# First attention of a two-block transformer kernel: a turned tile is copied ahead of the exponentials, a weight unit is split sooner, and the first weight load comes in two halves

## The reference, cut to what matters

```python
def dsa_mixer(h, w_in, kv_norm_g, w_uk, w_uv, w_o, rel_bias):
    q, c, qi, ki, wi = jnp.split(h @ w_in, ATT_IN_SPLITS, axis=-1)   # 16 heads of 64, latent 128
    c = rms_norm(c, kv_norm_g)
    q_lat = jnp.einsum('bshd,hdc->bshc', q, w_uk) * ATT_SCALE
    # for each of two blocks of 128 queries:
    dots = jax.nn.relu(jnp.einsum('bqhd,bsd->bqhs', qi_b, ki))       # 8 index heads
    score = jnp.einsum('bqh,bqhs->bqs', wi_b, dots)
    _, idx = lax.top_k(where(causal, score, -inf), 64)
    logits = q_lat_b . c_sel + rel_bias[t5_bucket(dist)]             # the 64 chosen keys only
    p = softmax(where(dist >= 0, logits, -inf))
    o_lat = p @ c_sel
    o = jnp.einsum('bshc,hcv->bshv', o_lat, w_uv)
    return o @ w_o
```

## Time and profile before

| | |
|---|---|
| Median of 3 runs | 875.04 us |
| The profiled execution's own time | 875.46 us |
| Its span, first to last instruction | 873.3 us |
| TensorE matmuls busy | 856.1 us (98%) |
| VectorE busy | 684.2 us (78%) |
| ScalarE busy | 474.7 us (54%) |
| GpSimd busy | 136.5 us (16%) |
| Mean granted TensorE clock | 0.996 |
| Share of TensorE in the chain that ended last | 93% |

### The profile page before, as it was taken

How to read it: one execution, slowest core, us unless ns; L and a number is a source line. 1 busy time by engine, 2 the same in 40 slices (tenths; PEclk the granted TensorE clock), 3 DMA queues, 4 the chain that set the end, 5 groups by cost and what they waited for, 6 DMA issues and landing times.

```text
span 873.3 us, 17948 instructions
## 1 busy us (share of the span) xinstructions
PE 856.1 (98%) x7016; PEld 816.8 (94%) x7016; DVE 684.2 (78%) x1074; ACT 474.7 (54%) x699; POOL 136.5 (16%) x154
## 2 busy tenths in 40 slices
PE   6999999999999998899999999999999999999998
PEld 5998999999999996699999999989899999999998
DVE  4897789898877797677666677677758998997884
ACT  7783455565443465765555444463367557645741
POOL 6230100014311000000000122232203223013000
PEclk9999999999999998999999999999999999999999
DMA  9755767769997450165665666566445544454652
GB/s 347 261 196 191 271 213 249 241 234 308 255 273 182 152 178 12 32 207 186 206 194 193 205 196 194 172 208 200 165 142 172 169 157 158 155 183 149 199 184 97
DMA packets 46960, 167.86 MB, mean 192 GB/s; under 512 B 5776, under 2 KB 5920, under 8 KB 46640
## 3 DMA queue, kind: packets, MB, share of 16 engines
q1 hardware_dynamic: 40896, 146.82, 50.7%
q0 software_dynamic: 5856, 20.00, 8.0%
q10 hardware_dynamic: 144, 0.15, 0.1%
HBM read 165.50 MB, written 1.44 MB: 191 GB/s over the span
## 4 chain that ended last, share of the span: by engine, by line
PE 93%; DVE 3%; ACT 2%; issue 1%; DMA 1%; POOL 0%; DVEq 0%; SPq 0%; ACTq 0%
PE bank L548 26%; PE bank L552 26%; PE bank L553 25%; PE bank L621 5%; PE bank L639 2%; PE bank L791 1%; PE bank L915 1%; PE bank L925 1%; PE bank L874 1%; PE bank L876 1%; PE bank L875 1%; DMA plain<-plain_w 1%; DVE lt L1736 1%; PE bank L782 1%; PE bank L803 0%
## 5 line engine op out<-in xcount | busy, mean ns | idle before, releaser
L1377 DVE TENSOR_TENSOR wlo<-raw,whi 128x1024 fp32r<-128x1024 f32 x260 | 319.5, 1261 | 91.8 <-ACT whi L1010 91.6
L552 PE MATMUL bank<-xl,whi 128*128 128x256 f32 x1328 | 370.1, 279 | 0.0
L553 PE MATMUL bank<-xh,wlo 128*128 128x256 f32 x1328 | 368.8, 278 | 0.0
L548 PE MATMUL bank<-xh,whi 128*128 128x256 f32 x1310 | 368.3, 281 | 0.0
L1010 ACT ACTIVATE whi<-raw 128x1024 fp32r<-128x1024 f32 x260 | 265.9, 1053 | 147.4 <-PE bank L553 135.8
L548 PEld LDWEIGHTS bank<-xh,whi 128*128 128x128 f32 x1310 | 246.0, 188 | 8.8 <-issue 6.8
L552 PEld LDWEIGHTS bank<-xl,whi 128*128 128x128 f32 x1328 | 249.6, 188 | 0.3
L553 PEld LDWEIGHTS bank<-xh,wlo 128*128 128x128 f32 x1328 | 249.5, 188 | 0.0
L552 PE MATMUL bank<-hlo,whi 128*128 128x256 f32 x512 | 141.9, 277 | 0.0
L553 PE MATMUL bank<-hhi,wlo 128*128 128x256 f32 x512 | 141.5, 276 | 0.0
L548 PE MATMUL bank<-hhi,whi 128*128 128x256 f32 x506 | 140.0, 277 | 0.0
(11 more groups left out here) (291 smaller groups left out, 1083.5 us busy)
## 6 DMA issues: line engine op xcount, KB each, us to landing
raw<-weights SPq DMA_DIRECT2D x260, 512.0 KB, 4.4
ada_raw<-ada_w POOLq DMA_DIRECT2D x24, 512.0 KB, 4.6
plain<-plain_w SPq DMA_DIRECT2D x16, 512.0 KB, 6.6
relB<-rel_scratch POOLq DMA_DIRECT2D x8, 256.0 KB, 7.3
bl<-rpb_in POOLq DMA_DIRECT2D x32, 64.0 KB, 3.4
x<-x_in SPq DMA_DIRECT2D x4, 256.0 KB, 6.3
cond<-cond_in POOLq DMA_DIRECT2D x1, 1024.0 KB, 7.5
cx<-ctx_in POOLq DMA_DIRECT2D x1, 1024.0 KB, 7.4
```

Source lines behind the costliest of these rows:

```text
L548: mmul(dst, hi, rh, start=start, stop=False)
L552: mmul(dst, hi, rlo, start=False, stop=False)
L553: return mmul(dst, lo, rh, start=False, stop=stop)
L1377: V_.tensor_tensor(wlo[:, sl], raw[:, sl], whi[:, sl].bitcast(F32), ALU.subtract)\
```

## The change

- **Start.** Plain chunk 0 is loaded in two halves with semaphores of their own, each 256 KB: the first behind x tiles 0 and 1, the second behind x tiles 2 and 3. TensorE waits for the first half at k = 0 and for the second at k = 4.
- **Ahead of the attention.** VectorE splits the two chunks of the second q unit while it would wait for the index weights and for the small transposition; before, it split them after the scores of block 0. Top-k rounds, scores and bank reads are put in another order behind it: three rounds of block 1 instead of two come before the loop. ScalarE's one-column Exp comes before its last split, not after it.
- **In the loop.** ScalarE's `copy_turned(g-2)` comes before `softmax(g)`. VectorE's top-k rounds are 1, 2, 1, 1 (the last after `queries(3)`) in g = 0, 1, 2, 2; before they were 1, 2, 1, 2. TensorE does three k steps of the output projection's first chunk at g = 12 and two at g = 13; before it did five at g = 13.

```diff
--- before.py
+++ after.py
@@ -270,7 +270,7 @@
         OUTS = (bank[7], bank[0])
 
 
-        names = """xg_ready plain_used cols_loaded consts_loaded rel_loaded w_hi_ready w_lo_ready chunk_used bank_emptied
+        names = """xg_ready plain_head plain_used cols_loaded consts_loaded rel_loaded w_hi_ready w_lo_ready chunk_used bank_emptied
             act_bank_emptied ada_used ada_summed cond_loaded cond_ready ones_ready x_hi_ready x_lo_ready x_squared tile_added
             squares_summed sum_in_psum root_ready rstd_ready dve_chain act_chain pool_chain rel_psum rel_table
             rel_stored rel_bias_loaded mask_ready bias2_ready k_full v_full kv_emptied gate_ready conv_ready rg_bank_read lam_parts lam_ready
@@ -336,8 +336,10 @@
                     sp.dma_start(raw[:, (2 * r + c) % 4], w[q * 8 + 2 * r + c]).then_inc(s_raw[(2 * r + c) % 4], 16)
 
             load_x(0)
-            load_plain(0)
-            for j in range(1, 4):
+            sp.dma_start(plain[:, 0, 0:CH // 2], plain_w[0][:, 0:CH // 2]).then_inc(S_["plain_head"], 16)
+            load_x(1)
+            sp.dma_start(plain[:, 0, CH // 2:CH], plain_w[0][:, CH // 2:CH]).then_inc(s_plain[0], 16)
+            for j in range(2, 4):
                 load_x(j)
             for n in range(1, 4):
                 load_plain(n)
@@ -614,8 +616,13 @@
                     pe.wait_ge(S_["bank_emptied"], f - 1)
                 for c in range(2):
                     n = N0[name] + 2 * unit + c
-                    pe.wait_ge(s_plain[n % NR], 16 * (n // NR + 1))
+                    if n:
+                        pe.wait_ge(s_plain[n % NR], 16 * (n // NR + 1))
                     for k in range(DT):
+                        if n == 0 and k == 0:
+                            pe.wait_ge(S_["plain_head"], 16)
+                        if n == 0 and k == DT // 2:
+                            pe.wait_ge(s_plain[0], 16)
                         if first_wait is not None and c == 0:
                             first_wait(k)
                         mm = mmul(b[:, c * S:(c + 1) * S], plain[:, n % NR, k * P:(k + 1) * P], rhs(k),
@@ -836,8 +843,10 @@
                     logits(g)
                 if g == 2:
                     q_last(1)
+                if g == NG:
+                    att_out_first(0, 0, 3)
                 if g == NG + 1:
-                    att_out_first(0, 0, 5)
+                    att_out_first(0, 3, 5)
                 if 2 <= g < NG + 2:
                     turn(pt, 3, "probs_ready", "turned_copied", "probs_turned", g - 2)
                 if g == NG + 2:
@@ -1183,8 +1192,8 @@
                     act.wait_ge(S_["dots_used"], g - 3)
                 A(rl[:, g % 4, 0:2 * n], DOTS[g % 4][:, 0:2 * n], ACT.Relu).then_inc(S_["dots_relu"], 1)
             ahead(U0["q"] + 2)
+            A(den[:, 0, 0:1], eps[:], ACT.Exp)
             ahead(U0["ukuv"])
-            A(den[:, 0, 0:1], eps[:], ACT.Exp)
 
             for j in range(4):
                 if j < 3:
@@ -1225,10 +1234,10 @@
                     half(U0["att_out"], 0)
                 if g == NG + 1:
                     half(U0["att_out"], 1)
+                if 2 <= g < NG + 2:
+                    copy_turned(g - 2)
                 if g < NG:
                     softmax(g)
-                if 2 <= g < NG + 2:
-                    copy_turned(g - 2)
                 if g >= 3:
                     act.wait_ge(S_["outs_full"], g - 2)
                     b, t0, nt, nk = GROUPS[g - 3]
@@ -1663,10 +1672,12 @@
                         .then_inc(S_["c_normed"], 1)
                 full(u)
                 emptied(V_.tensor_tensor(ci[:, 2 * j:2 * j + 2], two(bank[(F0["lat"] + j) % 2]), wide(R[:, 0]), ALU.mult))
+            half(U0["q"] + 1, 0)
             dve.wait_ge(S_["wi_psum"], 1)
             V_.scalar_tensor_tensor(wit[:], OUTB[0:2 * H_IDX, 0:S], IDX_SCALE, R[0:2 * H_IDX, 0], ALU.mult, ALU.mult)\
                 .then_inc(S_["wi_rows"], 1)
 
+            half(U0["q"] + 1, 1)
             dve.wait_ge(S_["wi_cols"], 1)
             ch.link(V_.tensor_copy(wi[:].rearrange("p b h -> p (b h)"), OUTB[:, S:S + QB * H_IDX]))
             def scores(g):
@@ -1705,23 +1716,22 @@
                 emptied(V_.scalar_tensor_tensor(qT[:, 2 * j:2 * j + 2], two(b), ATT_SCALE, wide(R[:, 0]), ALU.mult, ALU.mult))
             for g in range(4):
                 scores(g)
-            ahead(U0["q"])
-            topk(0, 0, 2)
+            topk(0, 0, 4)
             queries(0)
             dve.wait_ge(S_["c_hi"], 1)
             V_.tensor_tensor(cnl[:], cn[:], cnh[:].bitcast(F32), ALU.subtract).then_inc(S_["c_lo"], 1)
-            topk(0, 2, 4)
+            topk(0, 4, 5)
             ahead(U0["q"] + 1)
-            topk(0, 4, 8)
+            topk(0, 5, 8)
+            scores(4)
             queries(1)
+            scores(5)
             ahead(U0["q"] + 2)
-            scores(4)
-            scores(5)
+            scores(6)
             queries(2)
-            scores(6)
             scores(7)
             ahead(U0["ukuv"])
-            topk(1, 0, 2)
+            topk(1, 0, 3)
 
             def read_logits(g):
                 b, t0, nt, nk = GROUPS[g]
@@ -1763,13 +1773,13 @@
                 if 1 <= g <= NG:
                     norm_probs(g - 1)
                 if g == 0:
-                    topk(1, 2, 3)
+                    topk(1, 3, 4)
                 if g == 1:
-                    topk(1, 3, 5)
+                    topk(1, 4, 6)
                 if g == 2:
-                    topk(1, 5, 6)
+                    topk(1, 6, 7)
                     queries(3)
-                    topk(1, 6, 8)
+                    topk(1, 7, 8)
                 if g == 9:
                     half(U0["att_out"], 0)
                 if g == NG + 2:
```

## The result

The changed kernel takes **868.01 us** (median of 4 runs, 867.67 to 868.39) against 874.76 (4 runs, 874.32 to 875.98) of the kernel before on the same chip: 6.75 us less, a ratio of 0.992 with a 95% interval of 0.9905 to 0.9935. The forecast was 868.3. The profiled execution took 868.39 us with a span of 866.2; before they were 875.46 and 873.3.

What follows compares the result with a forecast made beforehand. TensorE was taken as the bound, so only its idle time and clock could be won. Terms 0.5 - 0.1 + 0.4 + 3.5 + 2.7 - 0.4 + 0.15 = 6.75 gave 868.3 us for the median, range 867.0 to 872.4.

Steps and rivals of the forecast that it cites:

- the mask: In the attention loop: mask 1.4 us sooner, PE's wait of 0.39 for it gone, +0.4 us.
- kT and the table: Ahead of the values: table load hidden in a ScalarE gap, kT copies 1.4 sooner, wait of 0.45 gone, +0.5 us.
- The copy ahead of the exponentials: In the attention loop: the transposition's waits for pT fall from 3.8 to 0.3 us, +3.5 (bounds 1.9 and 3.8).
- The added wait, costed at 0: ScalarE at g = 2: softmax(2) behind the copy ends near 336.3, VectorE wants it at 337.5; slack 1.2 us, cost 0.
- The clock: In the attention: with less PE idle time it keeps 2.4 GHz throughout, +2.7 us (bounds 0 and 2.9).
- the clock falls anyway: Rival: PE still idles in the attention, some 7 us run at 1.2 GHz, 871.0 us; chance 0.12.
- The wait for queries(3): PE's wait for the last q bank grows from 0.92 to 1.0 us, -0.1 (bounds -0.5 and +0.4).
- The end of the loop: Last hcl stands behind a VectorE split formerly finished in time; PE's wait grows 0.36 to 0.8, -0.4 us.
- The first load: At the start: halved load lets PE begin up to 0.7 us sooner, gain +0.15 (bounds 0 and 0.7).
- only the difference to POOL can be had: At the sum of squares: POOL runs 5.51 to 15.47, PE arrives at 15.69; that difference less 0.1 is the gain.
- The copy isn't what the transposition waits for: Rival: softmax(2) ends late, the transposition waits for VectorE's pt, wait only 1.90 to 0.7, 872.2 us; chance 0.08.
- The loop closes over one group: Rival: the next transposition needs the softmax behind the copy, 3.95 us a group, clock down, 881.3 us; chance 0.03.

Runs made afterwards that it cites:

- Experiment 1: Kernel before with only ScalarE's copy of the turned tile put ahead of the exponentials: 869.65 us against 874.94, ratio 0.9941.
- Experiment 5: Changed kernel again, 868.06 us; with its first weight load whole again, 868.50; with all five k steps at g = 13 again, 868.65.
- experiment 6: Changed kernel with five matmuls of the output projection's second unit cut in two by columns: 867.89 us, ratio 0.9924.
- experiment 2: Kernel before with only VectorE's whole list of the changed kernel (splits in two gaps, new order of rounds): 871.24 us, ratio 0.9962.
- experiment 3: Kernel before with 14 unused matmuls filling PE's wait ahead of the transposition of group 2: 873.86 us, ratio 0.999.
- experiment 4: Kernel before with only the first weight load in two halves: 873.76 us, ratio 0.9989.
- 7: Changed kernel with VectorE's queries(3) one top-k round sooner: 867.62 us against 867.61 of the changed kernel beside it.
- experiment 8: Changed kernel with the column cuts, q_last's two subtractions moved from VectorE to GpSimd, and rounds and queries(3) moved forward: 868.89 us, ratio 0.9937.

## Why the prediction was right

The mechanism was right where most of the gain lies, in the copy's place, the mask, kT and the table. The sum fits partly by luck, as the end of this section shows.

The prediction's steps against PE's timeline, each as how much sooner an instruction comes, before minus after. A step's gain is the difference to the one above:

| Instruction (PE's, the root ScalarE's) | before | after | sooner | step | forecast |
|---|---|---|---|---|---|
| first cnh matmul | 318.75 | 318.37 | 0.38 | start of the kernel 0.38 | 0.15 |
| first matmul of the values | 322.16 | 321.09 | 1.07 | kT and table 0.69 | 0.5 |
| mask of g = 3 | 335.42 | 334.72 | 0.70 | queries(3) -0.37 | -0.1 |
| mask of g = 4 | 338.14 | 336.97 | 1.17 | mask 0.47 | 0.4 |
| turn(2) | 341.14 | 338.21 | 2.93 | copy, first 1.76 | 1.75 |
| mask of g = 7 | 349.74 | 344.02 | 5.72 | clock 2.79 | 2.7 |
| mask of g = 11 | 359.46 | 352.98 | 6.48 | copy, later 0.76 | } 1.75 and |
| last waiting k step | 369.41 | 361.66 | 7.75 | copy and end 1.27 | } -0.4 |
| root of the next norm | 395.66 | 388.66 | 7.00 | pace -0.75 | none |

- **The copy ahead of the exponentials, 3.5 forecast.** 1.76 + 0.76 + 1.27 = 3.79, which still holds the end of the loop. The transposition was forecast for 338.5 and came at 338.21; the releaser was as worked out, with VectorE's norming done 0.06 ahead of it. Experiment 1 shows the condition that the prediction put on it: the copy pays in full only because VectorE is early too.
- **The added wait, costed at 0.** The Exps behind the first copy ended at about 335.4 (four of 0.39 from 333.89), earlier than the 336.3 worked out from the code's order, and VectorE took its tile at 337.27 without a gap. This step held.
- **The clock, 2.7.** It kept 1.00 and the profile gave 2.79. The rival "the clock falls anyway" didn't come in the three profiles of the kernel after, but it isn't refuted. Experiment 5's version with the k steps not moved lost 1.19 us to it behind the same 1.36 us. Of the 29 runs with this order of instructions in the attention up to g = 12 (those of the kernel after, of experiment 6 and of the two versions of experiment 5) two have a mean granted clock under 0.999: that one, and a run of the kernel after at 0.998 that took 869.52 us where the four others of its group took 867.24 to 867.89. The change makes the fall rare; it doesn't rule it out. The prediction also cites the Trainium skill, TensorE: Matmul & The Clock Gate, "A second HAM failure mode: psum-queue depth-cycling", a kernel in which small idle pieces alone made the clock swing. The traces are divided on it: experiment 2, with seven waits of 0.29 to 1.35 us between 335 and 360, stayed at 1.00 in all its windows, and the profile of experiment 5 fell behind a single listed wait. But the size is that of one execution. By experiment 3's times the clock is worth 0.1 to 1.7 us in the median, by the clocks of the 39 runs of the kernel before about 0.8, and experiment 4's low stretch was 3.4 us shorter. Against the medians the term is thus too large by 1 us or more; against the two profiles, where it was 2.79, it isn't. Which other step gives the median more than the profile isn't told apart.
- **kT and the table, 0.5.** 0.69. The wait of 0.45 isn't the whole cost of a wait: PE's matmuls start every 0.11 but last 0.28, so the idle time counts from the end of the last, and a wait costs up to 0.17 more than its row says; the matmul behind the wait also lasts 0.47 instead of 0.40. 0.45 + 0.17 + 0.07 = 0.69. The mask shows some of it too (0.47 for 0.39). The prediction called this "some latency" in one place and left it out elsewhere.
- **The wait for queries(3), -0.1.** -0.37, inside its bounds. The wait rose to 1.36, not 1.0. VectorE came 0.70 sooner as against 0.4 worked out, but PE came 1.07 sooner as against 0.5 + 0.15. The step that was mis-sized is PE's arrival.
- **The end of the loop, -0.4.** Wrong, it is 0: the wait is 0.35 now and was 0.36. The step held that the last hcl comes behind a split that "before was finished in time". It wasn't; in the kernel before, VectorE's rows show the split in that place already (after: 360.19 and 361.32, the same 1.13 apart):

```profile
367.94 1.22 DVE L1377 TENSOR_TENSOR wlo<-raw,whi 128x1024 fp32r<-128x1024 f32 x1
369.07 0.28 DVE L1754 TENSOR_TENSOR hcl<-bank,hch 128x128 fp32r<-128x128 f32 x1
```

  Reading these two rows ahead would have given 0.
- **The first load, 0.15.** The step "only the difference to POOL can be had" failed in its premise. POOL was to start at 5.51 as before; it started at 4.45, since x tiles 0 and 1 landed sooner:

```profile
4.45 1.03 POOL L394 TENSOR_TENSOR sqt<-x 128x512 f32<-128x512 f32 x1 [0.77 <-DMA x<-x_in]
...
13.01 1.33 POOL L395 TENSOR_TENSOR acc<-acc,sqt 128x512 f32<-128x512 f32 x1
...
15.28 0.41 PEld L609 LDWEIGHTS bank<-acc,ones 128*128 128x128 f32 x2
```

  POOL ends at 14.34, and PE reaches the sum of squares at 15.28 out of its own work: the sign that the prediction named as making it wrong. In other profiles POOL is what PE waits for, as forecast: with the load in halves PE's weight load for the sum starts 0.11 or 0.12 us behind POOL's end in four of eight (those of experiments 4, 7 and 8, and experiment 5's with the k steps not moved, where PE waits 0.8), and 0.39 to 0.94 behind it in the other four. So the 0.38 of the table isn't shown to be the load's. The first cnh matmul comes at 318.27 to 319.55 in the five profiles with the whole load and at 317.68 to 318.38 in the eight with halves; on one chip the whole one was at 318.27 and the kernel after at 318.38. By time the gain is 0.4 in experiment 5 and 1.2 in experiment 4, of which some is the clock's; its size stays open.
- **Not in the prediction at all:** the slow pace, -0.75. The prediction began with "only its idle time and its clock can be won", and put nothing down for a change of PE's own work; but the stretch of the same matmuls at the same clock took 27.00 us instead of 26.25. The steps above it gave 7.75 where 6.75 was forecast, and it takes 0.75 back. So the sum was met by errors of opposite sign, which is luck.
- **The rivals.** "The copy isn't what the transposition waits for" needs a late VectorE and is real in experiment 1, not in the change. "The loop closes over one group" is out: 2.24 us a group, and nothing waits.

Alone the copy, VectorE's list and the first load give 5.3, 3.7 and 1.2, which adds up to 10.2; the whole change gives 6.8. The copy and VectorE's list take away the same fall of the clock and shares of the same wait.

What stays open: what decides in an execution whether the clock falls and for how long (like waits gave 3.4 and 6.8 us; the same 1.36 us gave nothing and 3.4 us), and what in the order of PE's instructions picks the pace; that the three moved k steps do it is shown, why they do isn't.

## What to carry to other kernels

When an engine works on the products of two others in turn, put the step that only passes on a finished tile ahead of the long step that waits for the next one, and check that the other engine is early enough, or the wait changes its name only. Price a wait as its idle time plus the pipelined part of the next instruction, and a fall of the clock from the granted clocks of many runs, not from one profile. Where the last wait follows an engine without a gap, reordering that engine's list divides the wait and gains nothing.

## What the runs showed of the hardware

- **Two paces of the same matmul.** 128x256 matmuls with a weight load each start every 0.1133 or every 0.1178 us, both at 1.00 of the clock, for tens of microseconds. Matmuls cut by columns bring the fast one back (experiment 6).
- **The pace at the start.** In its first microseconds PE starts 3 to 4 matmuls a microsecond, later 6 to 7, though the record has the clock at 1.00 in both. When it steps up differs by execution, by up to 4 us (from 9 on in the profile without the moved k steps, from 13 on in that of experiment 3). The same microsecond in the kernel before and in experiment 3, whose start is the same:

```profile
12.00:13.00 1.00, 1.00 (x6) 0.88 (x5) 1.00 (x1) 1.00 (x3) 0.92 (x2) 1.00 1.03 410
```

```profile
12.00:13.00 1.00, 1.00 (x4) 0.82 (x3) 1.00 (x2) 1.00 (x4) 0.92 (x2) 1.00 1.02 406
```

  In the first PE had stepped up at 11, in the second it did so at 13, and the first mask matmul behind the last q bank came 0.8 later (336.22 against 335.42). Differences of 0.4 us at the start are under this.
- **The same wait, with and without a fall of the clock.** Behind 1.36 us of idle time the granted clock stayed at 1.00 in the six profiles of the kernel after, of experiment 6, of experiment 8 (1.33) and of experiment 5's whole first load, and fell to 0.50 for 3.4 us in one (experiment 5).
- **x sooner behind a smaller load.** POOL's first instruction, which waits for x tiles 0 and 1, started at 5.14 to 5.51 in five profiles with the whole 512 KB load behind them and at 4.45 to 5.05 in eight with half of it.
- **VectorE stands still behind GpSimd.** GpSimd's subtractions of 128x1024 elements took 2.52 and 2.38 us. A score update of VectorE's that began inside one took 2.52 and 1.89 us instead of 0.5 and ended 0.28 and 0.29 us after it; VectorE's read of a q bank, which lies between the two, took 0.69 as elsewhere (experiment 8). The Trainium skill, GPSIMD Engine Reference, "1. Specifications", says that GpSimd's interfaces to the on-chip memory are shared with VectorE, with contention when VectorE reads two inputs from there; the updates do, and the trace agrees. Here it cost VectorE more than the work handed over, 3.4 us against 2.4.
